# Moving the split operands of eight FFN phases to five other offsets in SBUF, five of them with their two parts side by side

## The chip, the cores and the metric

One core of one Trainium2 chip. The metric is the device time of one execution in microseconds, here the median of the runs shown. TensorE's granted clock is given as a share of 2.4 GHz.

## What is computed

A trunk of four layers on 256 tokens of 1024 features, all in float32. Each layer is FFN, mixer, FFN, each with a residual; the mixers are, in turn, forgetting attention (fox), a convolution module, differential attention, fox again. An FFN has 2816 hidden features:

```python
def _swiglu(h, w_gate, w_up, w_down):
    return (jax.nn.silu(h @ w_gate) * (h @ w_up)) @ w_down

for i in range(DEPTH):
    x = x + 0.5 * _swiglu(_rms_norm(x, norm_ffn1[i]), ffn1_w_gate[i], ffn1_w_up[i], ffn1_w_down[i])
    h = _rms_norm(x, norm_mix[i])
    y = (fox, conv, diff, fox)[i](h)
    x = x + y
    x = x + 0.5 * _swiglu(_rms_norm(x, norm_ffn2[i]), ffn2_w_gate[i], ffn2_w_up[i], ffn2_w_down[i])
```

## The kernel before

The program is one block per engine, each written out by hand in its own order, with semaphores between them. There are twelve phases, numbered 0 to 11: FFN, mixer, FFN for each of four layers, so that the FFN phases are 0, 2, 3, 5, 6, 8, 9 and 11.

**The split product.** A float32 product is made out of float32r ones. Each operand is the sum of a high part (the value copied as float32r) and a low part (the value less the high part). ScalarE makes the high parts, VectorE the low ones: of the weights at L470 and L808 (blocks of 128 x 2048 in a ring of five slots, sb_w_high and sb_w_low, fetched into sb_raw), of the normed input x at L488 and L852, of the hidden h at L552 and L983. The product is high x high + high x low + low x high; low x low is left out.

**TensorE in an FFN phase.** Weights are the stationary operand, x or h the moving one, tokens run along the columns. The two parts of x stand in one tensor, `x_both` [128, 2, 8, 256], and those of h in `h_both` [128, 2, 22, 256]: for tile k of 128 features the high part is `[:, 0, k, :]`, the low part `[:, 1, k, :]`. `on_both` (L1443) multiplies a tile of high weights with both parts at once, 512 columns, of which the access takes 256 from the one part and 256 from the other. `on_high` (L1448) multiplies a tile of low weights with the high part alone, 256 columns. `both_parts` issues for one output tile the 256-column ones of all k in a row, then the 512-column ones. Each matmul has a weight load of 128 columns of its own, beside the matmul before it.

`first_pair` and `one_pair` do gate and up: 11 pairs of blocks, 2 blocks a pair, 2 output tiles a block, 8 tiles k, so 352 matmuls of each width. `down` does the down projection: 4 output pairs, 2 tiles each, 22 tiles k in blocks of 8, 8 and 6, so 176 of each width. Even output tiles (n = 0) take the first 128 columns of a block's 256, odd ones (n = 1) the others, 512 bytes on. PSUM has eight banks of 512 columns; each output tile has one.

**The mixers** read x as well, high and low part apart, by `three_passes` (L1434 to L1436), 256 columns each, in `columns_half`, `tokens_half` and `first_block`. Their output projection reads `o_high` and `o_low` in the same way.

**Places.** Tensors are laid out in the order of their declaration. Two unused tensors, `shift_x` (16 elements) and `shift_h` (200 elements), stand ahead of `x_both` and `h_both`. In the built program, counted from a multiple of 1024 bytes, `x_both` begins at 192, `h_both` at 64, `o_high` and `o_low` at 320, and each weight tile at 128 (n = 0) or 640 (n = 1). `h_both` shares its bytes with the mixers' tensors.

Of the kernel before, what the change touches and what calls it, by code (L numbers as in the profile page):

```python
# [14 lines left out]
P = 128  # L15
# [25 lines left out]
TWO_PI_3 = 2.0 * math.pi - TWO_PI_1 - TWO_PI_2  # L41

# [16 lines left out]
def build_trunk(nc, A, out):  # L59
# [12 lines left out]
    with ExitStack() as ctx:  # L72
# [168 lines left out]
        def pair(t):  # L241
            return t.rearrange("p (a n) -> p a n", a=2)

# [217 lines left out]
        def _(act):  # L461
# [21 lines left out]
            def x_highs(i, T):  # L483
# [3 lines left out]
                for t in (2 * T, 2 * T + 1):  # L487
                    act.activation(x_high[:, t, :], xT[:, t, :], ACT.Copy, scale=vec[:, col + t:col + t + 1]  # L488
                                   ).then_inc(S["xhigh_ready"], 1)
# [46 lines left out]
            def ffn(i):  # L536
# [266 lines left out]
        def _(dve):  # L803
# [43 lines left out]
            def x_lows(i, T):  # L847

                col = NORM_COL + (i % 3) * DEPTH * KT + layer_of(i) * KT
                for t in (2 * T, 2 * T + 1):  # L850
                    dve.wait_ge(S["xhigh_ready"], 8 * i + t + 1)
                    dve.scalar_tensor_tensor(x_low[:, t, :], xT[:, t, :], vec[:, col + t:col + t + 1],  # L852
                                             x_high[:, t, :].bitcast(F32), ALU.mult, ALU.subtract
# [96 lines left out]
            def ffn(i):  # L950
# [30 lines left out]
                def low(p):  # L981
                    dve.wait_ge(S["h_high_ready"], PAIRS * f + p + 1)
                    dve.tensor_tensor(h_both[:, 1, 2 * p:2 * p + 2, :], pair(hidden[:, :]),  # L983
                                      h_both[:, 0, 2 * p:2 * p + 2, :].bitcast(F32),
# [447 lines left out]
        def _(pe):  # L1432
# [18 lines left out]
            def both_parts(at, n, high, low, m_both, ks, first, last):  # L1451
# [4 lines left out]
                for k in ks:  # L1456
                    on_high(at, n, low[:, k, :], m_both(k)[:, 0, :])
# [4 lines left out]
            def columns_half(dst, b, n, tiles=range(KT)):  # L1462

                high, low = (slot(t, b).rearrange("p (k n) -> p k n", k=KT) for t in (w_high, w_low))
                for k in tiles:
                    cols = slice(n * P, (n + 1) * P)
                    ins = three_passes(dst[:, n * SEQ:(n + 1) * SEQ], high[:, k, cols], low[:, k, cols],
                                       x_high[:, k, :], x_low[:, k, :], k == 0, k == KT - 1)
                return ins

            def tokens_half(dst, b, tt, tiles=range(KT)):
# [3 lines left out]
                for k in tiles:  # L1475
                    ins = three_passes(dst[:, tt * 256:(tt + 1) * 256], x_high[:, k, toks], x_low[:, k, toks],
# [28 lines left out]
            def first_block(i, dst):  # L1505
# [6 lines left out]
                for k in range(KT):  # L1512
                    pe.wait_ge(S["xlow_ready"], 8 * i + k + 1)
                    for n in range(2):
                        cols = slice(n * P, (n + 1) * P)
                        ins = three_passes(dst[:, n * SEQ:(n + 1) * SEQ], high[:, k, cols], low[:, k, cols],
                                           x_high[:, k, :], x_low[:, k, :], k == 0 and n == 0, k == KT - 1, True)
# [33 lines left out]
            def ffn(i):  # L1551
                b, f = starts[i], number(i)

                def tile(which, p, n, ks):
                    blk = b + 2 * p + which
                    high, low = (slot(t, blk).rearrange("p (k n) -> p k n", k=KT) for t in (w_high, w_low))
                    return both_parts(pair_banks(p) + 2 * which + n, n, high, low, lambda k: x_both[:, :, k, :],
                                      list(ks), ks[0] == 0, ks[-1] == KT - 1)

                def very_first_pair():  # L1560

                    for which in range(2):
# [3 lines left out]
                        for ks in (range(4), range(4, KT)):  # L1566
                            for k in ks:
                                pe.wait_ge(S["xlow_ready"], k + 1)
                                for n in range(2):
                                    on_both(at + n, n, high[:, k, :], x_both[:, :, k, :], k == 0, False)  # L1570
                            if which == 0 and ks[0] == 0:
                                wait_block(which)
                                for n in range(2):
                                    for k in ks:
                                        on_high(at + n, n, low[:, k, :], x_high[:, k, :])
                        wait_block(which)
                        for n in range(2):
                            for k in range(0 if which else 4, KT):
                                ins = pe.matmul(bank[at + n][:, SEQ:2 * SEQ], low[:, k, n * P:(n + 1) * P],
                                                x_high[:, k, :], start=False, stop=k == KT - 1, skip_group_check=True)  # L1580
# [25 lines left out]
                def down(T, c):  # L1606
# [9 lines left out]
                    for n in range(2):  # L1616
                        ins = both_parts(2 * (T % 2) + n, n, high, low, lambda k: h_both[:, :, first + k, :],
# [19 lines left out]
            def attention(i):  # L1637
# [88 lines left out]
                def fox_group(j, u=0):  # L1726
                    g = j - 1
                    q_blk, k_blk, v_blk = (b + 3 * j + n for n in range(3))
                    if j:
                        wait_block(q_blk)  # L1730
                        columns_half(bank[0], q_blk, 0)
                        columns_half(bank[0], q_blk, 1).then_inc(S["block_done"], 1)
# [5 lines left out]
                    columns_half(bank[1], k_blk, 0)  # L1738
                    columns_half(bank[1], k_blk, 1).then_inc(S["block_done"], 1)
# [9 lines left out]
                    tokens_half(bank[2], v_blk, 0, range(3))  # L1749
                    if j:  # L1750
                        score_pair(1, g, u)
                    tokens_half(bank[2], v_blk, 0, range(3, KT))
# [5 lines left out]
                    tokens_half(bank[2], v_blk, 1, range(2))  # L1758
                    if j:
                        head_sums("k", j, u)  # L1760
                    tokens_half(bank[2], v_blk, 1, range(2, 6))
# [3 lines left out]
                    tokens_half(bank[2], v_blk, 1, range(6, KT)).then_inc(S["block_done"], 1)  # L1765
# [4 lines left out]
                def diff_group(j, u=0):  # L1770
                    g = j - 1
                    q_blk, k_blk, v_blk = (b + 3 * j + n for n in range(3))
                    if j:
                        wait_block(q_blk)
                        columns_half(bank[0], q_blk, 0)
# [4 lines left out]
                        columns_half(bank[0], q_blk, 1).then_inc(S["block_done"], 1)  # L1780
# [5 lines left out]
                    columns_half(bank[1], k_blk, 0, range(ahead))  # L1786
                    if j:
                        head_sums("q", j, u)
                    if ahead < KT:
                        columns_half(bank[1], k_blk, 0, range(ahead, KT))  # L1790
                    columns_half(bank[1], k_blk, 1).then_inc(S["block_done"], 1)
# [9 lines left out]
                    tokens_half(bank[2], v_blk, 0)  # L1801
# [5 lines left out]
                    tokens_half(bank[2], v_blk, 1).then_inc(S["block_done"], 1)  # L1807
# [74 lines left out]
            def conv(i):  # L1882
                b = starts[i]
                for j in range(2 * GROUPS):
# [6 lines left out]
                    columns_half(bank[j % 4], b + j, 0)  # L1891
                    columns_half(bank[j % 4], b + j, 1).then_inc(S["block_done"], 1)
# [92 lines left out]
```

## Time and profile before

| what | us |
|---|---|
| median of two runs | 1986.67 (1984.39 to 1988.95) |
| span of the profiled execution | 1984.6 |
| TensorE busy in it | 1955.5 |
| VectorE busy | 1420.7 |
| ScalarE busy | 1044.4 |
| one FFN phase, 3 (510.7 to 693.7) | 183.0 |

The profile is one execution with the time of each instruction. "Busy" is the time in which an engine has at least one instruction under way. Matmuls overlap one another (the mean of one is longer than the distance to the next), so what a matmul costs is read from starts, not from durations. The line numbers are those of the kernel before.

### The profile page before, as it was taken

How to read it: one execution, taken by the hardware profiler on the slowest of the kernel's cores; microseconds unless marked ns; L12 is line 12 of the kernel's file. 1: busy time of each engine (PE TensorE's matmuls, PEld its weight loads, DVE VectorE, ACT ScalarE, POOL GpSimd, SP SyncE). 2: the span in 40 equal slices, each digit the busy share in tenths (PEclk: the TensorE clock that was granted, in tenths of full speed). 3: DMA queues.
4: the chain of work that ended last, by engine and by line, in shares of the span. 5: the costliest groups of instructions: out<-in, count | busy, mean ns of one | idle time of the engine just before them, and what ended most of it. 6: DMA issues, size and time to landing. Idle time of an engine off the chain costs nothing.

```text
span 1984.6 us, 29082 instructions
## 1 busy us (share of the span) xinstructions
PE 1955.5 (99%) x12574; PEld 1717.6 (87%) x12574; DVE 1420.7 (72%) x1645; ACT 1044.4 (53%) x1250; POOL 101.6 (5%) x114
## 2 busy tenths in 40 slices
PE   7999999999999998999999999999999999999999
PEld 6888889888888896988888888788888888888887
DVE  7776678875787565877587658887758765778763
ACT  6554566554555344654465455575436544566542
POOL 3000001000200001100100000010000000001000
PEclk9999999999999998999999999999999999999999
DMA  7655434655665683665656553356566655435653
GB/s 238 194 183 182 149 128 154 192 188 189 192 191 180 201 249 83 191 191 182 200 191 192 177 184 128 107 176 191 183 196 190 191 183 180 148 128 171 191 189 107
DMA packets 336365, 350.14 MB, mean 176 GB/s; under 512 B 10077, under 2 KB 331886, under 8 KB 336238
## 3 DMA queue, kind: packets, MB, share of 16 engines
q1 hardware_dynamic: 331742, 343.58, 54.1%
q10 hardware_dynamic: 4496, 4.70, 1.2%
q8 instruction: 99, 1.62, 0.3%
q14 instruction: 28, 0.23, 0.0%
HBM read 346.04 MB, written 2.22 MB: 175 GB/s over the span
## 4 chain that ended last, share of the span: by engine, by line
PE 94%; DVE 3%; ACT 2%; issue 1%; POOL 1%; DMA 0%; ACTq 0%; DVEq 0%; POOLq 0%
PE banks L1443 49%; PE banks L1448 24%; PE banks L1434 5%; PE banks L1436 5%; PE banks L1435 5%; PE banks L1901 1%; PE banks L1660 1%; PE banks L1713 1%; ACT sb_w_high L470 1%; DVE sb_w_low L808 1%; PE banks L1680 1%; PE banks L1697 1%; ACT sb_scores L598 0%; PE banks L1818 0%; PE banks L1667 0%
## 5 line engine op out<-in xcount | busy, mean ns | idle before, releaser
L808 DVE TENSOR_TENSOR sb_w_low<-sb_raw,sb_w_high 128x2048 fp32r<-128x2048 f32 (+1 forms) x332 | 749.5, 2262 | 208.8 <-ACT sb_w_high L470 208.2
L1443 PE MATMUL banks<-sb_x_both,sb_w_high 128*128 128x512 f32 x2816 | 721.9, 393 | 1.9 <-ACT sb_w_high L470 1.9
L470 ACT ACTIVATE sb_w_high<-sb_raw 128x2048 fp32r<-128x2048 f32 (+1 forms) x332 | 618.5, 1867 | 122.2 <-DMA sb_raw<-in_ffn_w_down 109.0
L1443 PEld LDWEIGHTS banks<-sb_x_both,sb_w_high 128*128 128x128 f32 x2816 | 500.2, 189 | 82.2 <-ACT sb_w_high L470 2.3
L1448 PEld LDWEIGHTS banks<-sb_x_both,sb_w_low 128*128 128x128 f32 x2792 | 386.5, 188 | 35.2
L1448 PE MATMUL banks<-sb_x_both,sb_w_low 128*128 128x256 f32 x2792 | 394.6, 279 | 0.0
L1443 PE MATMUL banks<-sb_h_both,sb_w_high 128*128 128x512 f32 x1408 | 360.2, 395 | 0.0
L1443 PEld LDWEIGHTS banks<-sb_h_both,sb_w_high 128*128 128x128 f32 x1408 | 250.8, 188 | 45.3
L1448 PEld LDWEIGHTS banks<-sb_h_both,sb_w_low 128*128 128x128 f32 x1408 | 190.9, 188 | 16.9
L1448 PE MATMUL banks<-sb_h_both,sb_w_low 128*128 128x256 f32 x1408 | 194.4, 279 | 0.0
L488 ACT ACTIVATE sb_x_both<-sb_xT,sb_vec 128x256 fp32r<-128x256 f32 x96 | 43.3, 501 | 200.8 <-DVE sb_xT L841 176.1
L1434 PE MATMUL banks<-sb_x_both,sb_w_high 128*128 128x256 f32 x512 | 147.1, 287 | 0.0
L543 ACT ACTIVATE sb_up_part<-banks 128x512 f32<-128x512 f32 x88 | 52.3, 595 | 174.9 <-PE banks L1443 174.9
L1436 PE MATMUL banks<-sb_x_both,sb_w_low 128*128 128x256 f32 x512 | 142.9, 279 | 0.0
L1435 PE MATMUL banks<-sb_x_both,sb_w_high 128*128 128x256 f32 x512 | 142.6, 279 | 0.0
L543 ACT ACTIVATE sb_gate_part<-banks 128x512 f32<-128x512 f32 x88 | 52.3, 594 | 163.6 <-PE banks L1443 163.6
L974 DVE TENSOR_TENSOR sb_up_part<-banks,sb_up_part 128x512 f32<-128x512 f32 x88 | 60.6, 689 | 59.1 <-ACT sb_up_part L543 59.1
L1434 PEld LDWEIGHTS banks<-sb_x_both,sb_w_high 128*128 128x128 f32 x512 | 96.1, 188 | 4.2 <-issue 4.0
L1435 PEld LDWEIGHTS banks<-sb_x_both,sb_w_high 128*128 128x128 f32 x512 | 96.4, 188 | 1.6 <-issue 1.4
L958 DVE TENSOR_TENSOR sb_gate_part<-banks,sb_gate_part 128x512 f32<-128x512 f32 x88 | 60.7, 690 | 51.2 <-ACT sb_gate_part L543 51.0
L1436 PEld LDWEIGHTS banks<-sb_x_both,sb_w_low 128*128 128x128 f32 x512 | 96.3, 188 | 0.0
L838 DVE SCALAR_TENSOR_TENSOR sb_xT<-banks,sb_xT 128x512 f32<-128x512 f32 x32 | 22.1, 691 | 97.1 <-PE banks L1443 97.1
(229 smaller groups left out, 1936.6 us busy)
## 6 DMA issues: line engine op xcount, KB each, us to landing
sb_raw<-in_ffn_w_gate SPq DMA_DIRECT2D x88, 1024.0 KB, 5.4
sb_raw<-in_ffn_w_up SPq DMA_DIRECT2D x88, 1024.0 KB, 5.3
sb_raw<-in_ffn_w_down SPq DMA_DIRECT2D x64, 1024.0 KB, 5.0
sb_raw<-in_ffn_w_down SPq DMA_DIRECT2D x32, 768.0 KB, 4.3
sb_raw<-in_fox_w_in SPq DMA_DIRECT2D x24, 1024.0 KB, 5.2
sb_raw<-in_conv_w_pw SPq DMA_DIRECT2D x12, 1024.0 KB, 5.4
sb_raw<-in_diff_w_in SPq DMA_DIRECT2D x12, 1024.0 KB, 5.0
sb_raw<-in_fox_w_out SPq DMA_DIRECT2D x8, 1024.0 KB, 4.8
```

The source lines that it names most:

```text
L470: act.activation(slot(w_high, b)[:, 0:width(b)], slot(raw, b)[:, 0:width(b)], ACT.Copy).then_inc(S["high_ready"], 1)
L488: act.activation(x_high[:, t, :], xT[:, t, :], ACT.Copy, scale=vec[:, col + t:col + t + 1]).then_inc(S["xhigh_ready"], 1)
L543: act.activation((up_part if which else gate_part)[:, :, :], banks[:, at:at + 2, SEQ:], ACT.Copy).then_inc(S["up_part_ready" if which else ...
L808: dve.tensor_tensor(slot(w_low, b)[:, 0:width(b)], slot(raw, b)[:, 0:width(b)], slot(w_high, b)[:, 0:width(b)].bitcast(F32), ALU.subtract) ...
L838: dve.scalar_tensor_tensor(xT[:, 2 * T:2 * T + 2, :], sums[:, :, SEQ:], 0.5, xT[:, 2 * T:2 * T + 2, :], ALU.mult, ALU.add).then_inc(S["x_h ...
L958: dve.tensor_tensor(gate_part[:, :, :], banks[:, at:at + 2, 0:SEQ], gate_part[:, :, :], ALU.add).then_inc(S["gate_sum_ready"], 1)
L974: dve.tensor_tensor(up_part[:, :, :], banks[:, at:at + 2, 0:SEQ], up_part[:, :, :], ALU.add).then_inc(S["up_sum_ready"], 1)
L1434: pe.matmul(dst, s_high, m_high, start=first, stop=False, skip_group_check=loose)
L1435: pe.matmul(dst, s_high, m_low, start=False, stop=False, skip_group_check=loose)
L1436: return pe.matmul(dst, s_low, m_high, start=False, stop=last, skip_group_check=loose)
L1443: return pe.matmul(pair(bank[at][:, :]), high[:, n * P:(n + 1) * P], m_both, start=first, stop=last, skip_group_check=True)
L1448: pe.matmul(bank[at][:, SEQ:2 * SEQ], low[:, n * P:(n + 1) * P], m_high, start=False, stop=False, skip_group_check=True)
```

## The change

Both tensors become flat with 256 elements to spare, the two shift tensors go, and two tables say for each FFN phase at which element its parts begin and whether they are side by side.

```diff
+X_PLACE = {0: (16, False), 2: (16, True), 3: (0, True), 5: (128, True), 6: (64, False), 8: (128, False),
+           9: (192, True), 11: (64, True)}
+H_PLACE = {0: (216, False), 2: (216, True), 3: (232, True), 5: (104, True), 6: (40, False), 8: (104, False),
+           9: (168, True), 11: (40, True)}
...
-        sb("shift_x", [P, 16])
-        x_both = sb("x_both", [P, 2, KT, SEQ], F32R)
-        x_high, x_low = x_both[:, 0, :, :], x_both[:, 1, :, :]
+        x_both = sb("x_both", [P, 2 * KT * SEQ + 256], F32R)
...
-        sb("shift_h", [P, 200])
...
-            h_both = during_ffn.enter_context(nc.sbuf_tensor("sb_h_both", [P, 2, FF_TILES, SEQ], F32R))
+            h_both = during_ffn.enter_context(nc.sbuf_tensor("sb_h_both", [P, 2 * FF_TILES * SEQ + 256], F32R))
...
+        def parts(buf, place, tiles):
+
+            at, together = place
+            flat = buf[:, at:at + 2 * tiles * SEQ]
+            if together:
+                return flat.rearrange("p (k a n) -> p a k n", a=2, n=SEQ)
+            return flat.rearrange("p (a k n) -> p a k n", a=2, n=SEQ)
+
+        def x_parts(i):
+            return parts(x_both, X_PLACE.get(i, (16, False)), KT)
+
+        def h_parts(i):
+            return parts(h_both, H_PLACE[i], FF_TILES)
+
+        def x_wide(i, k):
+            at, together = X_PLACE[i]
+            if together:
+                return x_both[:, at + 2 * k * SEQ:at + 2 * (k + 1) * SEQ]
+            return x_parts(i)[:, :, k, :]
...
-                    act.activation(h_both[:, 0, 2 * p:2 * p + 2, :], pair(hidden[:, :]), ACT.Copy
+                    act.activation(h_parts(i)[:, 0, 2 * p:2 * p + 2, :], pair(hidden[:, :]), ACT.Copy
...
-                return pe.matmul(pair(bank[at][:, :]), high[:, n * P:(n + 1) * P], m_both,
+                dst = bank[at][:, :] if len(m_both.shape) == 2 else pair(bank[at][:, :])
+                return pe.matmul(dst, high[:, n * P:(n + 1) * P], m_both,
...
-                    return both_parts(pair_banks(p) + 2 * which + n, n, high, low, lambda k: x_both[:, :, k, :],
-                                      list(ks), ks[0] == 0, ks[-1] == KT - 1)
+                    return both_parts(pair_banks(p) + 2 * which + n, n, high, low, lambda k: x_wide(i, k),
+                                      lambda k: x_parts(i)[:, 0, k, :], list(ks), ks[0] == 0, ks[-1] == KT - 1)
```

`h_wide` does for h what `x_wide` does for x. Every other use of `x_high`, `x_low`, `x_both[...]` and `h_both[...]` becomes the same part of `x_parts(i)` or `h_parts(i)`. Side by side, the high part of tile k is followed at once by its low part, and the 512 columns of `on_both` are one run; apart, they lie as before. The writes of h, two tiles at once, are one run of 512 where the parts are apart and two runs of 256 where they are side by side; those of x are one tile of 256 either way.

In the built program the beginnings of x and of h come to lie as follows, counted from a multiple of 1024 bytes:

| phase | parts | x | h |
|---|---|---|---|
| 0 | apart | 192 | 64 |
| 2 | side by side | 192 | 64 |
| 3 | side by side | 128 | 128 |
| 5 | side by side | 640 | 640 |
| 6 | apart | 384 | 384 |
| 8 | apart | 640 | 640 |
| 9 | side by side | 896 | 896 |
| 11 | side by side | 384 | 384 |

The weight tiles stay at 128 and 640. The mixers' x stays at its place, and `o_high` and `o_low` go from 320 to 480. The tensors between move by 960 bytes. No engine has an instruction more, less, or elsewhere in its order.

## Rows read from the trace of the kernel before

**Rows 1.** The page: busy us, share of the span, instructions; granted clock in 40 slices.

```profile
PE 1955.5 (99%) x12574; PEld 1717.6 (87%) x12574; DVE 1420.7 (72%) x1645; ACT 1044.4 (53%) x1250; POOL 101.6 (5%) x114
...
PEclk9999999999999998999999999999999999999999
```

**Rows 2.** Waits of TensorE in the whole span: us, times, longest.

```profile
PE banks L1944 <- DMA sb_wide<-in_norm_ffn: 7.1, 1, 7.1
PE banks L1434 <- DVE sb_o_low L1360: 5.4, 1, 5.4
PE banks L1680 <- DVE sb_scores L1103: 4.6, 5, 1.2
PE banks L1907 <- DVE sb_hidden L1305: 2.2, 1, 2.2
PE banks L1443 <- ACT sb_w_high L470: 1.9, 1, 1.9
PE banks L1531 <- DVE sb_xT L841: 1.5, 1, 1.5
PE banks L1498 <- POOL sb_square_sum L407: 1.2, 1, 1.2
PE banks L1660 <- DVE sb_kT L1057: 1.0, 1, 1.0
PE banks L1434 <- DVE sb_o_low L1128: 0.9, 1, 0.9
```

**Rows 3.** Windows, phase 6 gate and up, then down: us, busy (instructions), clock, DMA.

```profile
987.10:1108.80 121.70, 121.70 (x707) 1.00 0.59 190
1108.80:1170.10 61.30, 61.30 (x353) 1.00 0.58 191
```

**Rows 4.** Lines by form in 987.1 to 1108.7 and 1108.7 to 1170.1, TensorE.

```profile
L1443 PE MATMUL banks<-sb_x_both,sb_w_high 128*128 128x512 f32 x352 | 90.2, 392 | 0.0
L1448 PE MATMUL banks<-sb_x_both,sb_w_low 128*128 128x256 f32 x352 | 49.8, 278 | 0.0
L1498 PE MATMUL banks<-sb_square_sum,sb_ones 128*128 128x256 f32 x2 | 0.6, 378 | 0.0
...
L1443 PE MATMUL banks<-sb_h_both,sb_w_high 128*128 128x512 f32 x176 | 45.0, 395 | 0.0
L1448 PE MATMUL banks<-sb_h_both,sb_w_low 128*128 128x256 f32 x176 | 24.3, 279 | 0.0
```

**Rows 5.** Windows over FFN phases 2, 3, 5, 6, 8 and 9, columns as above.

```profile
327.50:510.70 183.20, 183.20 (x1061) 1.00 0.59 189
510.70:693.70 183.00, 183.00 (x1059) 1.00 0.59 190
804.00:987.10 183.10, 183.10 (x1061) 1.00 0.59 189
987.10:1170.10 183.00, 183.00 (x1059) 1.00 0.59 190
1303.20:1486.40 183.20, 183.20 (x1061) 1.00 0.59 189
1486.40:1669.50 183.10, 183.10 (x1060) 1.00 0.60 190
```

**Rows 6.** Timeline of TensorE, gate and up: start us, us, instructions merged.

```profile
1001.57 1.07 PE L1448 MATMUL banks<-sb_x_both,sb_w_low 128*128 128x256 f32 x8
1002.48 1.99 PE L1443 MATMUL banks<-sb_x_both,sb_w_high 128*128 128x512 f32 x8
1004.31 1.11 PE L1448 MATMUL banks<-sb_x_both,sb_w_low 128*128 128x256 f32 x8
1005.25 2.00 PE L1443 MATMUL banks<-sb_x_both,sb_w_high 128*128 128x512 f32 x8
1007.08 0.28 PE L1448 MATMUL banks<-sb_x_both,sb_w_low 128*128 128x256 f32 x1
```

**Rows 7.** Timeline of TensorE, down part.

```profile
1119.97 0.85 PE L1448 MATMUL banks<-sb_h_both,sb_w_low 128*128 128x256 f32 x6
1120.66 1.56 PE L1443 MATMUL banks<-sb_h_both,sb_w_high 128*128 128x512 f32 x6
1122.06 0.85 PE L1448 MATMUL banks<-sb_h_both,sb_w_low 128*128 128x256 f32 x6
1122.74 1.79 PE L1443 MATMUL banks<-sb_h_both,sb_w_high 128*128 128x512 f32 x7
1124.37 1.11 PE L1448 MATMUL banks<-sb_h_both,sb_w_low 128*128 128x256 f32 x8
1125.31 2.03 PE L1443 MATMUL banks<-sb_h_both,sb_w_high 128*128 128x512 f32 x8
```

**Rows 8.** Sixteen passes on sb_xT: timeline, then lines by form with its mean.

```profile
208.24 3.63 PE L1818 MATMUL banks<-sb_xT,sb_gate_w_gained 128*16 128x256 f32 x16
...
L1818 PE MATMUL banks<-sb_xT,sb_gate_w_gained 128*16 128x256 f32 x16 | 3.6, 380 | 0.0
```

**Rows 9.** Lines by form: matmuls on o_high and o_low.

```profile
L1434 PE MATMUL banks<-sb_o_high,sb_w_high 128*128 128x256 f32 x256 | 74.9, 293 | 6.3 <-DVE sb_o_low L1360 5.4 <-DVE sb_o_low L1128 0.9
L1435 PE MATMUL banks<-sb_o_low,sb_w_high 128*128 128x256 f32 x256 | 72.2, 282 | 0.0
L1436 PE MATMUL banks<-sb_o_high,sb_w_low 128*128 128x256 f32 x256 | 72.2, 282 | 0.0
```

**Rows 10.** By source line: writes of h and of x, duration ns min/median/max.

```profile
L552 ACT ACTIVATE sb_h_both<-sb_hidden x88: 613/619/640, 36.8 to 1919.3; 128x512 fp32r<-128x512 f32 x88
...
L983 DVE TENSOR_TENSOR sb_h_both<-sb_hidden,sb_h_both x88: 681/683/687, 38.9 to 1921.6; 128x512 fp32r<-128x512 f32 x88
...
L488 ACT ACTIVATE sb_x_both<-sb_xT,sb_vec x96: 491/496/514, 9.2 to 1796.7; 128x256 fp32r<-128x256 f32 x96
```

More of the change, by code:

```diff
@@ L1449, in on_high, with both_parts @@
                           start=False, stop=False, skip_group_check=True)
-            def both_parts(at, n, high, low, m_both, ks, first, last):
+            def both_parts(at, n, high, low, m_both, m_high, ks, first, last):
                 for k in ks[:1]:
@@ L1456, in both_parts @@
                 for k in ks:
-                    on_high(at, n, low[:, k, :], m_both(k)[:, 0, :])
+                    on_high(at, n, low[:, k, :], m_high(k))
                 for k in ks[1 if first else 0:]:
@@ L1460, in both_parts, with columns_half @@
                 return ins
-            def columns_half(dst, b, n, tiles=range(KT)):
+            def columns_half(i, dst, b, n, tiles=range(KT)):
                 high, low = (slot(t, b).rearrange("p (k n) -> p k n", k=KT) for t in (w_high, w_low))
@@ L1467, in columns_half, with tokens_half @@
                     ins = three_passes(dst[:, n * SEQ:(n + 1) * SEQ], high[:, k, cols], low[:, k, cols],
-                                       x_high[:, k, :], x_low[:, k, :], k == 0, k == KT - 1)
+                                       x_parts(i)[:, 0, k, :], x_parts(i)[:, 1, k, :], k == 0, k == KT - 1)
                 return ins
-            def tokens_half(dst, b, tt, tiles=range(KT)):
+            def tokens_half(i, dst, b, tt, tiles=range(KT)):
                 high, low = (slot(t, b).rearrange("p (k n) -> p k n", k=KT) for t in (w_high, w_low))
@@ L1569, in very_first_pair @@
                                 for n in range(2):
-                                    on_both(at + n, n, high[:, k, :], x_both[:, :, k, :], k == 0, False)
+                                    on_both(at + n, n, high[:, k, :], x_wide(i, k), k == 0, False)
                             if which == 0 and ks[0] == 0:
@@ L1574, in very_first_pair @@
                                     for k in ks:
-                                        on_high(at + n, n, low[:, k, :], x_high[:, k, :])
+                                        on_high(at + n, n, low[:, k, :], x_parts(i)[:, 0, k, :])
                         wait_block(which)
@@ L1616, in down @@
                     for n in range(2):
-                        ins = both_parts(2 * (T % 2) + n, n, high, low, lambda k: h_both[:, :, first + k, :],
+                        ins = both_parts(2 * (T % 2) + n, n, high, low, lambda k: h_wide(i, first + k),
+                                         lambda k: h_parts(i)[:, 0, first + k, :],
                                          list(range(last - first)), c == 0, c == len(DOWN) - 1)
@@ L1764, in fox_group @@
                         turn(3, g, u)
-                    tokens_half(bank[2], v_blk, 1, range(6, KT)).then_inc(S["block_done"], 1)
+                    tokens_half(i, bank[2], v_blk, 1, range(6, KT)).then_inc(S["block_done"], 1)
                     if j:
@@ L1774, in diff_group @@
                         wait_block(q_blk)
[L1775 removed]
+                        columns_half(i, bank[0], q_blk, 0)
                         if j > 1:
@@ L1785, in diff_group @@
                     ahead = KT if j == 1 else 2
-                    columns_half(bank[1], k_blk, 0, range(ahead))
+                    columns_half(i, bank[1], k_blk, 0, range(ahead))
                     if j:
@@ L1789, in diff_group @@
                     if ahead < KT:
-                        columns_half(bank[1], k_blk, 0, range(ahead, KT))
-                    columns_half(bank[1], k_blk, 1).then_inc(S["block_done"], 1)
+                        columns_half(i, bank[1], k_blk, 0, range(ahead, KT))
+                    columns_half(i, bank[1], k_blk, 1).then_inc(S["block_done"], 1)
                     if j:
```

49 lines of the change are left out of this document (28 added, 21 removed).

## The prediction

> **What bounds the kernel now.** I read the busy times first [rows 1]: TensorE is busy for 99% of the span, VectorE for 72%, ScalarE for 53%, at a granted clock of 1.00 in nearly every slice. Then TensorE's waits [rows 2]: what it waited for adds up to 25.8 us in 1984.6, the largest of it ahead of the first matmul and in the mixers; on a tile of an FFN phase only 1.9 us, once, at the very start. So an FFN phase is a queue of matmuls without a hole, and its time is the number of matmuls times the distance from one start to the next. The windows over phase 6 say the same [rows 3]: 121.7 us for the gate and up part, 61.3 us for the down part, TensorE busy throughout, with 352 + 352 and 176 + 176 matmuls in them [rows 4].
>
> The mean of 392 ns in those rows is no distance, since matmuls overlap. The timeline gives it: the start of a group of eight less the start of the next. On x, eight of 512 columns take 1.83 us both times (1002.48 to 1004.31, 1005.25 to 1007.08), so **228.8 ns each**; eight of 256 take 0.91 us in one group and 0.94 us in the next, **113.8 and 117.5 ns** [rows 6]. On h, 512 columns take 1.40 us for six and 1.63 us for seven, **233 ns**, and the three groups of 256 take 0.69 and 0.68 us for six and 0.94 for eight: 115, 113 and 117.5 ns, mean 115.3 [rows 7]. Check: 352 x (228.8 + 115.7) = 121.3 us, plus two passes of the sum of squares; 176 x (233 + 115.3) = 61.3 us. The account closes on [rows 3], and all FFN phases but the first and the last, which hold other waits, take 183.0 to 183.2 us [rows 5].
>
> **The change, part by part.** Instructions added or removed: none, on any engine; no wait and no DMA moves. The mixers keep x at its present address.
>
> *Side by side (phases 2, 3, 5, 9, 11).* A 512-column matmul now reads two runs of 256, which lie 8 KB (x) or 22 KB (h) apart; side by side it reads one run of 512. If the surplus is a price per run, one run saves the difference between the 512 and the 256 surplus: 6.5 ns on x, 11.1 on h, or 352 x 6.5 + 176 x 11.1 = 4.2 us a phase and 21 us in five. If it is a price per column (stalls that come in proportion to what is read), the same two numbers fit as well, and it saves nothing. The rows of before can't tell, because all its 256-column matmuls have one run and all its 512-column ones have two. Far bound: only the yardstick's 3.4 ns stays, 352 x 12.1 + 176 x 16.3 = 7.1 us a phase, 36 us in five. I take **-8 us**, below the middle of 0 and 21: that h pays 4 ns more than x on 512 columns and nothing more on 256 speaks for some price of the far second run, but for no more than a part.
>
> The Trainium skill ("TensorE: Matmul & The Clock Gate", Back-to-back issue gap) gives N/2.4 + 2.5 ns, 215.8 and 109.2 ns, which this trace exceeds by 13 to 17 ns and 4 to 8 ns. By that rule, met once the runs are joined, the five phases would save about 38 us.
>
> *Other offsets (phases 3, 5, 6, 8, 9, 11).* Counted from a multiple of 1024 bytes, each weight tile begins at 128 or 640. Now x begins at 192 and h at 64, 64 bytes from the first of these. In the six phases both go to 128 (phase 3), 640 (5, 8), 384 (6, 11) or 896 (9): either the weights' own residue or 256 bytes from it. That place matters at all is read from [rows 6]: two neighbouring groups with the same moving operand, engine and count differ by 3.7 ns a matmul, and their weights' residue is one of the things that differ (640 in the first, 128 in the second). That it isn't residue alone is seen in [rows 7], where the first group, with weights at 128, takes 115 and the third, also at 128, 117.5. Bounds from the levels seen: all at the cheapest (228.8 and 113.5): x -0.7, h -1.1, so -1.8 us a phase, -11 in six; all at the dearest (233 and 117.5): x +2.1, h +0.4, +2.5 us a phase, +15 in six. A start that coincides with the weights' is outside what the trace shows, and I expect that to be worse rather than better, so I take **+4 us**.
>
> *Mixers' o_high and o_low* move by 160 bytes, 320 to 480 from a multiple of 1024. 768 matmuls [rows 9] by at most 4 ns is 3 us either way; I take 0.
>
> *ScalarE's and VectorE's h instructions.* In five phases the 55 high parts and 55 low parts write two runs of 256 in place of 512 in a row. Now they take 619 and 683 ns; two of 256 would be about 2 x 496 (the x instruction, [rows 10]), so at worst +0.37 us each, 4 us a phase on each engine. They lie beside TensorE: the pair's product is needed by the down part alone, and ScalarE is idle for 47% and VectorE for 28% of the span [rows 1]. Cost 0. Were the cover gone, only the last pair's 0.37 us times two would stand ahead of the down part, 4 us in five phases.
>
> Sum on the profiled execution: 1984.6 - 8 + 4 = 1980.6 us. The runs' median is 1986.67, 2.1 above this span, so the forecast is **1982.7 us**.
>
> **The rivals.**
> *N, nothing changes (0.12).* The moving operand and the weights are fetched without regard for each other, and the surplus is per column. For it: the even 183 us of six FFN phases [rows 5]. Against it: 3.7 ns between the groups of [rows 6]. Time 1986.7. The Trainium skill ("SBUF — State Buffer", Who interferes with whom) states this: TensorE has two independent read ports and never waits on anyone. The trace doesn't agree in so far as the two groups differ.
> *B, one run saves the whole run price (0.20).* For it: 15.5 is not far from twice 9.0. -21 us and offsets near 0: 1965.
> *C, the weights' residue costs (0.26).* Moving data and weights are kept 64 bytes off each other now. Suppose that the two reads hinder each other where they stand at the same residue: in phases 3, 5 and 8 they would start there, for half of the weight tiles. For it: [rows 6], and h, which sits on the other side of 128, pays 4 ns more on 512. Against it: x and h hardly differ on 256 columns, and the groups of [rows 7] differ at one residue. If the six phases' surplus grows by a third, 13.6 / 3 x 6 = +27 us, less some 4 for the joined runs: 2010. The point from which it decides: the gain of 8 us is gone at 1.3 us a phase, 1.2 ns on each of 1056 matmuls, and the kernel is 2% slower at 6.6 us a phase, 6.3 ns on each.
> *D, the writes in two runs come to the front (0.04).* +4 us to a few more, if ScalarE or VectorE falls behind the weight blocks: about 1995.
> *E, all goes to the yardstick (0.02).* -36 us and -11: 1940.
>
> **How the numbers follow.** My own case, small terms of both signs, has the remaining 0.36, with 1974 to 1996 as its range; it is the likeliest, so its time is the prediction. The range must reach into B and C: 1962 (B with a few us from the offsets) to 2016 (C with 5 us a phase). About 2 in 10 stay outside, mostly above. Two per cent is 39.7 us, about what a measurement of this kernel can tell from no change. Faster by that only in E and the tail of B: 0.03. Slower by it in the upper quarter of C: 0.07. Within: 0.90.
>
> **What would show it.** The start-to-start distance, phase by phase. Phase 2 has the old places joined: if 512 columns fall from 228.8 to about 222 and h from 233 to 222, the price is per run; if they stay, per column; I expect 2 to 4 ns less. Phases 6 and 8 are apart and differ from phase 0 by place alone: phase 8 above phase 6 speaks for C. Phase 3 against phase 2 gives the place with both joined. The distance of x's 256-column matmuls should stay between 113 and 118. TensorE's waits should stay near 26 us, and the mixers within 1 us each. A new wait of TensorE on sb_h_both or on sb_w_low, or a phase of 190 us or more or 176 or less, would make the prediction wrong.

## The result and the profile after

The changed kernel takes 2003.11 us (2001.59 to 2004.62, two runs), 1.0084 times as long as before, interval 1.0051 to 1.0117. Timed once more beside the kernel before, in five runs, it took 2001.91 us against 1987.88, ratio 1.0071, 1.0057 to 1.0085. The forecast was 1982.7: the time went the other way. It is inside the range and within two per cent.

The page of the changed kernel, busy times and granted clock, answers to [rows 1]:

```profile
PE 1971.4 (98%) x12574; PEld 1731.2 (86%) x12574; DVE 1422.8 (71%) x1645; ACT 1044.7 (52%) x1250; POOL 99.3 (5%) x114
...
PEclk9999999999999998999999999999999999999999
```

TensorE is busy 15.9 us longer with the same 12574 matmuls, at a clock that the 40 slices show as the same; the span grows by 18.2 us to 2002.8. Its waits (answering to [rows 2]; us, times, longest) grow from 25.8 to 28.1 us. None is new, but two are longer: on sb_hidden in the convolution phase (2.2 to 3.3 us) and on sb_square_sum in phase 0 (1.2 to 2.5 us):

```profile
PE banks L1976 <- DMA sb_wide<-in_norm_ffn: 7.0, 1, 7.0
...
PE banks L1939 <- DVE sb_hidden L1333: 3.3, 1, 3.3
PE banks L1528 <- POOL sb_square_sum L435: 2.5, 1, 2.5
PE banks L1472 <- ACT sb_w_high L498: 1.9, 1, 1.9
```

Most of the growth is that the matmuls stand further apart. The windows over phase 2 (first two lines), phase 3 (next two) and phase 6 (last two), gate and up first and then down, columns as in [rows 3]:

```profile
330.20:452.00 121.80, 121.80 (x708) 1.00 0.60 188
452.00:513.30 61.30, 61.30 (x353) 1.00 0.59 189
513.30:636.70 123.40, 123.40 (x708) 1.00 0.59 188
636.70:698.20 61.50, 61.50 (x354) 1.00 0.59 190
996.10:1119.40 123.30, 123.30 (x707) 1.00 0.59 188
1119.40:1180.90 61.50, 61.50 (x353) 1.00 0.58 190
```

Phase 2, whose parts are side by side at the old places, has its old length. Phases 3 (side by side) and 6 (apart) both have grown, to 123.4 and 61.5 us from 121.7 and 61.3, with the same instructions. The timeline of phase 6, gate and up, answers to [rows 6]:

```profile
1010.74 1.12 PE L1477 MATMUL banks<-sb_x_both,sb_w_low 128*128 128x256 f32 x8
1011.70 2.00 PE L1472 MATMUL banks<-sb_x_both,sb_w_high 128*128 128x512 f32 x8
1013.54 1.11 PE L1477 MATMUL banks<-sb_x_both,sb_w_low 128*128 128x256 f32 x8
1014.49 1.78 PE L1472 MATMUL banks<-sb_x_both,sb_w_high 128*128 128x512 f32 x7
```

512 columns take 1.84 us for eight, 230 ns (228.8 before). Both 256-column groups now take 0.95 to 0.96 us for eight, 119 to 120 ns (113.8 and 117.5 before). The down part answers to [rows 7]:

```profile
1127.84 1.12 PE L1477 MATMUL banks<-sb_h_both,sb_w_low 128*128 128x256 f32 x8
1128.79 2.00 PE L1472 MATMUL banks<-sb_h_both,sb_w_high 128*128 128x512 f32 x8
1130.63 0.88 PE L1477 MATMUL banks<-sb_h_both,sb_w_low 128*128 128x256 f32 x6
1131.34 1.55 PE L1472 MATMUL banks<-sb_h_both,sb_w_high 128*128 128x512 f32 x6
1132.73 0.88 PE L1477 MATMUL banks<-sb_h_both,sb_w_low 128*128 128x256 f32 x6
```

Here 512 columns have become cheaper, 1.84 us for eight and 1.39 for six, 230 to 232 ns (233 before), and 256 columns dearer, 0.95 us for eight and 0.71 for six, 118 to 119 ns (115.3 on average before).

Each of the phases 3, 5, 6, 8, 9 and 11 is 1.6 to 1.8 us longer, from its first matmul on x to the end of its down part, whichever of the four offsets it has and whether its parts are joined or not: 10.3 us in all. The other 7.9 us of the profiled span are in phase 0 (1.55 us) and the four mixers. The windows of the mixers, fox, conv, diff and fox, before:

```profile
201.90:327.50 125.60, 125.60 (x1017) 1.00 0.43 136
693.80:804.00 110.20, 102.59 (x1101) 0.95 0.62 170
1170.10:1303.20 133.10, 126.26 (x936) 1.00 0.40 128
1669.50:1794.90 125.40, 125.40 (x1017) 1.00 0.43 136
```

and in the changed kernel:

```profile
203.40:330.20 126.80, 126.80 (x1018) 1.00 0.42 135
698.20:811.30 113.10, 104.42 (x1101) 0.94 0.60 166
1180.90:1314.80 133.90, 127.06 (x935) 1.00 0.39 127
1684.40:1811.40 127.00, 127.00 (x1017) 1.00 0.42 135
```

Behind the 0.95 and 0.94 of the second lines, the convolution phase, stand stretches at a granted clock of 0.50, the lower of TensorE's two levels (1.2 and 2.4 GHz). The 40 slices are too coarse to show them. In the kernel before, from 29.6 to 33.0 us (phase 0) and twice in the convolution phase:

```profile
29.60:33.00 3.40, 3.40 (x22) 1.00 0.22 54
759.70:763.10 3.40, 3.40 (x36) 0.50 0.00 0
776.80:783.60 6.80, 4.13 (x19) 0.50 0.00 0
```

and in the changed kernel:

```profile
29.60:33.00 3.40, 3.40 (x12) 0.50 0.48 158
763.50:770.30 6.80, 5.66 (x46) 0.50 0.00 0
784.00:790.80 6.80, 4.62 (x22) 0.50 0.01 2
```

In phase 0 TensorE has just waited 2.5 us for the sum of squares (1.2 us before), and of the matmuls that follow 12 start in 3.4 us in place of 22: that is the 1.55 us of phase 0. In the convolution phase 13.6 us are at 0.50 in place of 10.2. So part of the growth is no matter of places.

### The profile page after: what moved, and what is told of

Its sections match the earlier page's. It is cut to its first block, busy times and chain, and to the rows that moved or that the text cites. A ratio compares the mean times of both kernels' runs of the same rounds, so it can differ in the third digit from the quotient of the medians.

```text
span 2002.8 us, 29082 instructions
## 1 busy us (share of the span) xinstructions
PE 1971.4 (98%) x12574; PEld 1731.2 (86%) x12574; DVE 1422.8 (71%) x1645; ACT 1044.7 (52%) x1250; POOL 99.3 (5%) x114
## 4 chain that ended last, share of the span: by engine, by line
PE 92%; DVE 3%; ACT 2%; DMA 2%; issue 1%; POOL 1%; ACTq 0%; SPq 0%; DVEq 0%; POOLq 0%
PE banks L1472 48%; PE banks L1477 25%; PE banks L1462 5%; PE banks L1463 4%; PE banks L1464 4%; DMA u_away<-sb_u_pad 1%; PE banks L1692 1%; PE banks L1745 1%; ACT sb_w_high L498 1%; PE banks L1933 1%; PE banks L1712 1%; DVE sb_w_low L836 1%; PE banks L1729 1%; DMA sb_raw<-in_ffn_w_gate 0%; ACT sb_scores L626 0%
## 5 line engine op out<-in xcount | busy, mean ns | idle before, releaser
L1477 PE MATMUL banks<-sb_x_both,sb_w_low 128*128 128x256 f32 x2792 | 400.3, 281 | 0.0
L1464 PE MATMUL banks<-sb_x_both,sb_w_low 128*128 128x256 f32 x512 | 142.8, 279 | 0.0
```

Source lines behind the costliest of these rows:

```text
L1464: return pe.matmul(dst, s_low, m_high, start=False, stop=last, skip_group_check=loose)
L1477: pe.matmul(bank[at][:, SEQ:2 * SEQ], low[:, n * P:(n + 1) * P], m_high, start=False, stop=False, skip_group_check=True)
```

## The experiments

In the following, d is the distance from the beginning of a weight tile to the beginning of the moving operand, modulo 256 bytes. Weight tiles begin at 128 and 640, which is the same modulo 256. So x had d = 64 and h d = 192 before, and the changed kernel gives both d = 0 in four of its offsets: 128, 384, 640 and 896 differ by multiples of 256. Of the title's five offsets the fifth (192 for x, 64 for h) is the old one: six phases move, and all six to the same d. A phase's length is counted from its first matmul on x to its first on h (gate and up), and from there to the next phase's first matmul (down); phases 0 and 11 are left out for h, and phase 0 for x, since other work stands in them.

### The layout alone

```diff
+X_PLACE = {0: (0, True), 2: (0, True), 3: (0, True), 5: (0, True), 6: (0, True), 8: (0, True), 9: (0, True), 11: (0, True)}
+        sb("shift_x", [P, 16])
+        x_both = sb("x_both", [P, 2 * KT * SEQ + 0], F32R)
```

H_PLACE is the same table, and shift_h stands ahead of h_both again, which has no spare elements either.

> The kernel before, with the two parts of x and h side by side in all eight FFN phases, every tensor beginning at its old address. Theory P (place alone matters: the moving operand's start counted in 128 bytes): no effect, 1986.7 us within 1 us, phase 2's windows 121.6 and 61.1 us as in the changed kernel. Theory L (the layout matters and phase 2 was an exception): slower or faster by 2 us or more over eight phases. My old case B would give 1965.

Measured: 1986.96 us against 1987.12, ratio 0.9997, 0.9988 to 1.0006. Phase 3 in its windows:

```profile
510.65:632.40 121.75, 121.75 (x707) 1.00 0.60 190
632.40:693.70 61.30, 61.30 (x353) 1.00 0.58 189
```

The old lengths, with all eight phases side by side. A 512-column matmul pays 229.0 ns on x and 232.8 on h whether it reads one run or two. The surplus is no price per run (the whole effect lies between -2.4 and +1.2 us), and the step of 4 ns between x and h has nothing to do with the 22 KB between h's parts. As expected by theory P; my case B is out.

### The allocation alone

```diff
+X_PLACE = {0: (16, False), 2: (16, False), 3: (16, False), 5: (16, False), 6: (16, False), 8: (16, False), 9: (16, False), 11: (16, False)}
+H_PLACE = {0: (216, False), 2: (216, False), 3: (216, False), 5: (216, False), 6: (216, False), 8: (216, False), 9: (216, False), 11: (216, False)}
```

> The changed kernel's allocation (x_both and h_both with 256 spare elements, no shift tensors), but all eight phases apart at the old offsets, so that x is at its old bytes, h 1024 bytes further, and all tensors behind x are moved by 960 or 160 bytes as in the changed kernel. Theory P with its remainder: of the 18 us, 10.5 belong to the six phases at new places and go; about 8 stay in the mixers and at the start, from o_high and o_low at 480 and the tensors moved along: 1994 to 1995 us. Rival (everything hangs on the FFN phases, the mixers' growth comes from them): 1986 to 1988.

Measured: 1989.88 us, ratio 1.0015, 1.0005 to 1.0024: +2.8 us, not +8. All FFN phases from 2 on have their old lengths, so the 10 us do belong to the six phases' places. What is left for the allocation is less than the profile of the changed kernel led me to think. The convolution phase of these executions explains a part: it took 107.6 us in the run with the layout alone, 109.0 here, 110.3 before, 113.2 in the first profile of the changed kernel, and in its second profile, with the same program:

```profile
698.10:807.20 109.10, 101.24 (x1101) 0.97 0.62 172
```

A stage that moves by 4 us from one execution to the next can't be charged to a change from one profile. What it moves with is the granted clock. In the thirteen profiles of this case the phase takes 107.6 to 109.9 us where 6.8 us of it are at 0.50, 108.9 to 111.5 us where 10.2 are, and 112.4 to 113.2 us where 13.6 are.

### o_high and o_low alone

```diff
-        sb("shift_o", [P, 24])
+        sb("shift_o", [P, 64])
```

This is the kernel before with that one line changed, the size of a third unused tensor, which stands ahead of o_high; u_pad, behind o_low, moves along by the same 160 bytes.

> The kernel before with o_high and o_low alone moved by 160 bytes, from 320 to 480 (d from 192 to 96), as the changed kernel has them. Theory R: their 768 matmuls go from 115.6 to 120.0 ns as in the changed kernel, +3.4 us, 1990.5. Rival (the mixers' growth came from other tensors or from the transfers of the convolution phase): within 1 us of 1987.

Measured: 1990.04 us against 1987.16, ratio 1.0014, 1.0004 to 1.0023, +2.9 us, as much as the whole allocation. The distances from start to start of the output projections' matmuls (those under 160 ns, so without the waits) have a mean of 119.9 ns, against 115.6 before. For 768 matmuls that makes 3.3 us, which the interval (0.8 to 4.6 us) holds. So the allocation's cost is that of these matmuls, whose d went from 192 to 96.

### The weights moved instead

```diff
+        sb("shift_w", [P, 16])
         with ExitStack() as landing:
...
-        sb("shift_x", [P, 16])
```

> The kernel before with 64 bytes ahead of the weight tensors and none ahead of x: the weight tiles begin at 192 and 704 in place of 128 and 640, and x, h, o_high, o_low keep their old addresses (xT and x_square move by 64 too). If the distance between moving operand and weights decides (theory R), both are now at the same residue mod 64 and 128, as in the changed kernel's six phases: 256 columns at 118.8 ns, 512 at 230.4, gate and up 123.1 us, all phases and mixers, +15 to +20 us, 2002 to 2007. If the moving operand's own place decides (theory P): 121.6 us a phase, 1986 to 1988.

Measured: 2009.88 us, ratio 1.0124, 1.0107 to 1.0141, +22.8 us, though x, h and o keep every one of their old addresses. The timeline of phase 6, gate and up:

```profile
1013.25 1.11 PE L1477 MATMUL banks<-sb_x_both,sb_w_low 128*128 128x256 f32 x8
1014.21 2.00 PE L1472 MATMUL banks<-sb_x_both,sb_w_high 128*128 128x512 f32 x8
1016.05 1.12 PE L1477 MATMUL banks<-sb_x_both,sb_w_low 128*128 128x256 f32 x8
1017.00 2.00 PE L1472 MATMUL banks<-sb_x_both,sb_w_high 128*128 128x512 f32 x8
```

Read as in [rows 6]: 0.96 and 0.95 us for eight of 256, 1.84 and 1.83 us for eight of 512, the changed kernel's distances. Here x at 192 has d = 0, as x at 128 had there, and gate and up takes 123.3 us in both. h at 64 now has d = 128, and its down part takes 61.84 us, which is also what h takes at d = 128 in the next experiment (61.81). At these places the moving operand's own place decides nothing; its distance from the weights does. Theory P falls. The time is 3 us over the expected 2007: I had priced h at d = 0, 61.5 us, and at d = 128 it takes 0.35 us more, eight times. The profiled execution also has 3.4 us at half clock in phase 0, about 1.5 us. Not shown is what in the weights' tensors matters. DMAs, ScalarE and VectorE write them while TensorE reads them, and all of that moved together; that the distances repeat from group to group within 0.2 ns speaks for TensorE's own regular reads.

### Sixteen distances

Three programs, each profiled in one execution, give x and h a place of their own in each phase; the second, for instance:

```diff
+X_PLACE = {0: (16, False), 2: (0, False), 3: (4, False), 5: (8, False), 6: (12, False), 8: (20, False), 9: (24, False), 11: (28, False)}
+H_PLACE = {0: (16, False), 2: (20, False), 3: (24, False), 5: (28, False), 6: (0, False), 8: (4, False), 9: (8, False), 11: (12, False)}
```

> One look: parts apart in all phases; x begins at 192, 128, 256, 320, 384, 448, 512, 576 (counted from a multiple of 1024 bytes) in phases 0, 2, 3, 5, 6, 8, 9, 11, and h at 640, 576, 704, 768, 832, 896, 960, 1024. The weights stay at 128 and 640. If the period is 128 bytes (0 against 64): gate and up 123.1 us in phases 2, 3, 6 and 9 and 121.5 in 5, 8 and 11; down 61.3 in phases 3, 5, 6... wherever h is a multiple of 128 (768, 896, 1024: phases 5, 8, 11) and 61.1 at 576, 704, 832, 960. If it is 256: some of the places not tried so far (256 and 512 for x, 704 and 960 for h) show a third value.

> One look, steps of 16 bytes. With d the distance from a weight tile's beginning to the moving operand's, modulo 256: x at d = 64, 0, 16, 32, 48, 80, 96, 112 in phases 0, 2, 3, 5, 6, 8, 9, 11, h at 128, 144, 160, 176, 64, 80, 96, 112; o_high and o_low at d = 64. Theory R (d modulo 256 sets the stalls): x 123.1 us at 0 and the values between run from there to 121.6 at 64 and on toward 123.8 at 128; h 60.7 at 64, 61.6 at 128. Rival R64 (only the 64-byte step counts, what lies within is the same): plateaus, so 123.1 at 16, 32, 48 and 121.6 at 80, 96, 112; h 61.6 at 144 to 176 and 60.7 at 80 to 112.

> One look, the other half: x at d = 192, 128, 144, 160, 176, 208, 224, 240 in phases 0, 2, 3, 5, 6, 8, 9, 11, h at 0, 16, 32, 48, 192, 208, 224, 240. Theory R: x 123.8 at 128 down to 122.3 at 192 and back to 123.1 at 0; h 61.3 at 0, 60.7 near 48, 61.1 at 192. Rival R64: x 123.8 at 144 to 176, 122.3 at 208 to 240; h 61.3 at 16 to 48, 61.1 at 208 to 240.

Measured in the first program, windows over gate and up of phases 3 (d = 128), 5 (192), 6 (0) and 8 (64):

```profile
512.60:636.60 124.00, 124.00 (x708) 1.00 0.59 186
808.70:931.20 122.50, 122.50 (x708) 1.00 0.60 187
993.00:1116.40 123.40, 123.40 (x708) 1.00 0.60 187
1310.70:1432.60 121.90, 121.90 (x708) 1.00 0.59 188
```

Phases 9 and 11 repeat 3 and 5 with x 256 bytes further and give the same to 0.1 us (124.0 and 122.5), so the period of 256 holds at the places tried; a third value does appear, so it isn't 128. All three programs together, in us (the 61.3 and 61.5 of h at 192 and 0 are those of the other kernels too):

| d | 0 | 16 | 32 | 48 | 64 | 80 | 96 | 112 |
|---|---|---|---|---|---|---|---|---|
| gate and up (x) | 123.3 | 123.0 | 123.6 | 123.1 | **121.9** | 123.7 | 124.7 | 123.6 |
| down (h) | 61.5 | 61.3 | 61.6 | 61.8 | **60.9** | 61.7 | 62.2 | |

| d | 128 | 144 | 160 | 176 | 192 | 208 | 224 | 240 |
|---|---|---|---|---|---|---|---|---|
| gate and up (x) | 124.0 | 123.8 | 124.0 | 124.2 | 122.5 | 125.1 | 124.2 | 123.8 |
| down (h) | 61.8 | 61.6 | 61.9 | 62.1 | 61.3 | 62.2 | 61.8 | |

Neither a smooth curve nor plateaus of 64 bytes, so both expectations miss. Nor is d = 0, where the two beginnings coincide, a dear place: for x four distances are cheaper and eleven dearer. For x there are two dips, at 64 and at 192, and 16 bytes beside them most of the gain is lost. For h the lowest is 64 as well, with 192 level with 16 and 0.8 to 0.9 us below its neighbours 176 and 208. Before, x stood in the better dip and h in the other; the changed kernel leaves both in six phases. The place is worth at most 3.2 us in 122 for x. Each distance but those of the kernels timed was seen in one or two phases of one execution; a phase repeats to 0.2 us from one profile to the next.

### h moved to the better distance

```diff
+H_PLACE = {0: (32, False), 2: (32, False), 3: (32, False), 5: (32, False), 6: (32, False), 8: (32, False), 9: (32, False), 11: (32, False)}
```

The rest stands at the addresses of the kernel before; h_both has 32 elements to spare.

> The kernel before with h alone moved by 128 bytes in all eight phases, from d = 192 to d = 64. Theory R: down part 60.7 instead of 61.1 us, eight times, -3.2 us, 1983.9. The changed kernel's own reason (the moving operand's place without regard to the weights) gives no number here; if nothing changes, R is wrong for h: 1987.

Measured: 1984.67 us against 1987.16, -2.5 us, ratio 0.9988, 0.9979 to 0.9998. The timeline of the down part in phase 6, to be read beside [rows 7]:

```profile
1122.72 0.84 PE L1477 MATMUL banks<-sb_h_both,sb_w_low 128*128 128x256 f32 x6
1123.40 1.54 PE L1472 MATMUL banks<-sb_h_both,sb_w_high 128*128 128x512 f32 x6
1124.78 0.84 PE L1477 MATMUL banks<-sb_h_both,sb_w_low 128*128 128x256 f32 x6
1125.46 1.76 PE L1472 MATMUL banks<-sb_h_both,sb_w_high 128*128 128x512 f32 x7
```

512 columns take 1.38 us for six and 1.60 for seven, 229 to 230 ns instead of 233, and 256 columns 0.68 us for six. Over the whole part the means are 229.4 ns (232.8 before) and 116.4 ns (115.6 before). The phase is 0.45 us shorter, 3.5 us in eight; the interval holds 0.4 to 4.2 us.

### Fewer weight columns loaded

```diff
+LOADED = {0: 128, 2: 128, 3: 96, 5: 64, 6: 32, 8: 64, 9: 32, 11: 128}
...
+                m = P if first else LOADED[phase_now[0]]
-                return pe.matmul(dst, high[:, n * P:(n + 1) * P], m_both,
+                return pe.matmul(dst[0:m], high[:, n * P:n * P + m], m_both,
```

`on_high` is cut down in the same way. In the trace a load of 32 columns lasts 108 ns and one of 128 columns 188.

> One look. The kernel before, but the matmuls of the FFN phases load fewer of a tile's 128 weight columns: 96 in phase 3, 64 in phases 5 and 8, 32 in phases 6 and 9, all 128 in 0, 2 and 11; the first matmul of each output tile loads all 128 everywhere. The moving side is untouched; the output rows beyond the loaded columns miss their sums, so part of the computation is left out. Theory W (the surplus is the moving read held up by the weight load that runs beside it): on x the 15.5 and 9.0 ns shrink about in proportion, 512 columns 229 at 128, near 221 at 64, near 217 at 32; 256 columns 115.8, 111, 109. Rival M (the moving read has its own cost): 229 and 115.8 in all phases.

Measured, phase 6 with 32 columns loaded, gate and up:

```profile
1005.09 2.01 PE L1476 MATMUL banks<-sb_x_both,sb_w_high 128*32 128x512 f32 x8
1006.94 1.10 PE L1482 MATMUL banks<-sb_x_both,sb_w_low 128*32 128x256 f32 x8
1007.87 2.01 PE L1476 MATMUL banks<-sb_x_both,sb_w_high 128*32 128x512 f32 x8
1009.72 1.09 PE L1482 MATMUL banks<-sb_x_both,sb_w_low 128*32 128x256 f32 x8
```

Eight of 512 take 1.85 us, 231 ns, and eight of 256 0.93 and 0.92 us, 116 ns; gate and up is 122.7 us long, against 121.8 with 128 columns. With 96 columns it is 123.9, with 64 it is 122.3 and 122.4. The surplus does not shrink with the columns loaded, so theory W falls in its simple form. It isn't rival M either, since the length of the load changes the distances, by up to 4 ns: on x both widths become dearer, on h 512 columns become cheaper (232.8 to 230.6 with 96). So the load has a part in the surplus and does not set its amount. What the bulk of it is (on x 15.7 ns on 512 columns at d = 64, and 7.5 on 256 at d = 192, the lowest means seen) stays open.

### A better version

```diff
+        sb("shift_w", [P, 32])
         with ExitStack() as landing:
...
         w_low = sb("w_low", [P, RING, 2048], F32R)
+        sb("shift_high", [P, 32])
```

Each of the two shifts is 128 bytes. w_low begins at a multiple of 256 with this and w_high 128 bytes beyond one, as before; everything behind w_high moves on by 256 bytes, and h by 128 more, as in the experiment on h.

> Meant as the better version. Each stream gets the distance that the looks at 64 and 16 bytes found cheapest: w_high stays at d = 64 below x (512 columns, 229.0 ns), w_low moves to a multiple of 256 so that x is at d = 192 from it (256 columns, 114.2 ns in place of 115.8), h goes to d = 64 from w_high. Everything else moves by 256 bytes. If the distance to the weights whose matmul is under way or next decides within each group (theory R in full): gate and up 121.0 us, down 60.4, -0.6 and -0.7 a phase, with the mixers 1975 to 1979. If only w_high's distance counts or the two can't be parted: no better than h alone moved, 1984.

Measured: 1981.54 us against 1987.88, ratio 0.9969, 0.9957 to 0.9980. It beats both kernels, by 6.3 us over the one before. Its gate and up part, phase 6:

```profile
1000.22 2.01 PE L1474 MATMUL banks<-sb_x_both,sb_w_high 128*128 128x512 f32 x8
1002.06 1.08 PE L1479 MATMUL banks<-sb_x_both,sb_w_low 128*128 128x256 f32 x8
1002.98 2.00 PE L1474 MATMUL banks<-sb_x_both,sb_w_high 128*128 128x512 f32 x8
1004.82 1.07 PE L1479 MATMUL banks<-sb_x_both,sb_w_low 128*128 128x256 f32 x8
```

The 256-column groups on x take 0.92 and 0.91 us, so both are at the cheap level now, at which the first of the three programs had them with x at d = 192 (114.2 ns): the low weights' distance can be set apart from that of the high weights. But the 512-column ones went from 229.0 to 229.8 on average, and on h the split lost a little on 512 (230.3 against 229.4) and gained as much on 256. Gate and up took 121.65 us on average, 0.15 less than before, and down 60.89, 0.42 less; over eight phases that makes 4.6 of the 6.3 us (interval 4.0 to 8.5). The rest isn't placed: three mixers have their old lengths to 0.3 us, and phase 0 (1.0 us longer, with 3.4 us at half clock) and the convolution phase move with the clock. So I had the gain of the phases at more than twice its size, and the time at 1975 to 1979.

### The changed kernel again

> The changed kernel once more, timed beside the kernel before on one chip. From the parts: 10.5 us from the six phases' places and 3.4 us from o_high and o_low at d = 96, so 2001; the rest of the first 18 us (1.5 in phase 0, 2.9 in the convolution phase) is change between executions and averages out. If it doesn't: 2003 to 2005.

Measured: +14.0 us (ratio 1.0071), 2001.91. The parts, 10.3 for the FFN phases and 2.9 for the output projections, make 13.2, which is 1.0066 and inside the interval. In this execution, too, gate and up takes 123.3 us in each of the six phases, and down 61.5 in the five that end in no other work.

## Why the prediction was wrong

**What bounds the kernel** was right: an FFN phase is a queue of matmuls without a hole, its time the number of matmuls times their distance. The writes of h in two runs cost nothing at all, as ScalarE's row over all 88 shows, five phases of eight in two runs, against 619 in [rows 10]:

```profile
L580 ACT ACTIVATE sb_h_both<-sb_hidden x88: 611/618/634, 36.7 to 1937.2; 128x512 fp32r<-128x512 f32 x88
```

**The term for side by side is the one that failed.** I took -8 us between 0 and -21 for reading one run of 512 columns in place of two of 256, and it is 0 (experiment on the layout: -0.2 us, interval -2.4 to +1.2). The reason I gave, that h pays 4 ns more than x on 512 columns and nothing more on 256, has another cause: h was at d = 192 and x at d = 64. At d = 192 x pays the same 232.6 ns, and at d = 64 h pays 229.4. I had an observation with two candidate causes, distance between the parts and place, counted it for the first and priced the second on its own. Without this term the forecast would have been +4, of the right sign and a quarter of the 16.4 us measured.

**The term for the offsets** was right in kind and within its bounds of -11 to +15, but taken at +4 where it measured +10.3. Its sign was luck in part: I expected a start that coincides with the weights' to be worse for coinciding, and no row of before had one. The scan shows that d = 0 is an ordinary distance (123.3 us, among 123.0 to 125.1). What the changed kernel lost is the dip at d = 64, 121.8 us, in which x stood without my knowing it. The list of places misled me: I counted modulo 1024 and saw four new offsets, "the weights' own residue or 256 bytes from it"; counted modulo 256 there is one, d = 0. And the two groups of [rows 6], weights at 128 and at 640, have the same d. So their 3.7 ns, from which I took that place matters, are no effect of that distance: with x 256 bytes further, in the first of the three programs, groups alternate between the same two levels, and at d = 0 all take 119 ns. The lower level goes with the odd output tiles (n = 1). What makes the difference no run tests.

**The mixers** were bounded at 3 us either way and taken as 0; o_high and o_low cost 2.9. The bound was good, the middle was not.

**The rivals.** C, the weights' residue, comes nearest: place relative to the weights counts. But it had the cost in phases 3, 5 and 8, for half of the weight tiles, from reads at one residue; all six phases pay the same 1.6 to 1.8 us, and one residue is no dear distance. Its size was a third of the surplus, 27 us; measured it is 1.7 us of 13.6 a phase, an eighth. N is refuted by the weights moved alone. It was the rule of the Trainium skill ("SBUF — State Buffer", Who interferes with whom) that TensorE's two read ports are independent and it never waits on anyone; here 64 bytes in the distance between the two operands are worth 22.8 us in 1987. B and E did not come: one run of 512 columns still takes 229 ns and not the 215.8 that the Trainium skill gives for a matmul by itself ("TensorE: Matmul & The Clock Gate", Back-to-back issue gap).

**The signs.** Phase 2 stayed at 229.0 and 232.8 ns on 512 columns, where I expected 2 to 4 ns less. x's 256-column matmuls left the stretch of 113 to 118 (118.8 on average), and the mixers grew by 0.8 to 2.9 us instead of less than 1. Phase 8 above phase 6 was to speak for C; the two are alike to 0.1 us (184.8), because 640 and 384 have the same distance modulo 256.

**What lay outside the six phases**: 7.9 us of the profiled growth. About 3 are the output projections. About 3 are TensorE's clock, which I had at nothing: 1.55 us in phase 0, and up to 1.7 us in the convolution phase, for 3.4 us more at half clock. The rest, between 1 and 2 us, isn't placed. Phase 0's gate and up takes 126.2 us in six profiles, which have no half clock after the sum of squares, and 127.7 to 127.8 in four, which have 3.4 us of it there, all with x at d = 64. In those four (both profiles of the changed kernel, the allocation alone, h moved) TensorE had waited 2.5 to 3.3 us for that sum just before, and in the six 1.2 to 2.5 us. Whether the change or chance decides this, no run tests.

## What to carry to other kernels

Where a TensorE-bound kernel reads both operands of float32r matmuls at full rate, their places can be worth a per cent, as here: count the distance between moving and stationary tile modulo 256 bytes and keep it when something is inserted or padded ahead of either, because 64 bytes ahead of the weights alone cost 1.2% here. Which distance is good has to be measured: the one where the two coincide was neither the worst nor good. Such a scan is cheap if each phase of one program gets a place of its own, since the trace then gives the time of one distance per phase. Before charging a few microseconds to a change, read the granted clock in stretches of a few microseconds, not in slices of 50. And when one observation fits two terms of a sum, price it in both before choosing either.

## What was not expected of the hardware

The time from one matmul's start to the next depends here on where the moving tile lies relative to the weight tile, modulo 256 bytes, with two narrow dips for x at 64 and 192 (121.9 and 122.5 us of gate and up against 123.0 to 125.1 elsewhere). It does not depend on whether 512 columns are one run or two (229.0 ns both ways). Groups of the same kind take 113.8 or 117.5 ns for 256 columns at d = 64, and with x at d = 192 from the low weights nearly all take the lower one (114.5 on average); what picks the level at d = 64 isn't known. Why there is a surplus over 213.3 and 106.7 ns at all, and why loading 32 weight columns instead of 128 doesn't remove it, isn't settled here.
